# Two operand buffers of a TensorE kernel start 32 bytes lower in their partition

## The chip, the core and the metric

The kernel runs on one core of a Trainium2 chip. The metric is the device time of one execution in microseconds. Three runs of the kernel before took 1187.24 to 1188.97 us, median 1188.03 us.

## The reference

Two transformer-like blocks run one after the other over one sequence of 256 tokens with 1,024 features, all in fp32.

```python
# first block
u = rms_norm(h, norm_mix)
z, xbc, dt_raw, q_a, c_kv, k_rope, gate_ssd, gate_mla = split_cols(u @ w_in, IN_SPLITS)
y_ssd = ssd_branch(z, xbc, dt_raw, ...) @ w_ssd_out
y_mla = mla_branch(q_a, c_kv, k_rope, positions, ...) @ w_mla_out
h = h + (sigmoid(gate_ssd) * y_ssd + sigmoid(gate_mla) * y_mla) @ w_o
h = h + memory_cross_attention(rms_norm(h, norm_xattn), rms_norm(mem, norm_mem), ...)
h = h + hierarchical_moe(rms_norm(h, norm_moe), ...)     # 32 experts, top 2 of one group
x = rms_norm(h, norm_final)
# second block
hq, hf, hi, hg, sq, sk, sv = split(rmsnorm(x, attn_pre_norm) @ w_in_2)
mix = concatenate([rmsnorm(hgrn2_mix(hq, hf, hi)) * silu(hg), rmsnorm(stick_breaking_mix(sq, sk, sv))]) @ w_out_2
h = x + rmsnorm(mix, attn_post_norm)
gate, up = split(rmsnorm(h, ffn_pre_norm) @ w_gate_up_2)
h = h + rmsnorm((silu(gate) * up) @ w_down_2, ffn_post_norm)
out = h + (p @ ple_proj_2) * sigmoid(h @ ple_gate_2)
```

## The kernel before

Activations lie with features on the 128 partitions and tokens along them: a buffer of the shape [128, 8, 256] holds 8 groups of 128 features of all 256 tokens, so one row of 256 tokens is 1,024 bytes of a partition. The large products are made with three matmuls in place of one. A factor x is split into an upper part, x rounded to the format fp32r, and a lower part, the rest; ScalarE (ACT) writes the upper part by a copy (line 1180) and VectorE (DVE) the lower one by a subtraction (line 1757 for weights, 1763 for activations). The product is upper by upper, plus weight upper by activation lower, plus weight lower by activation upper.

Weights come in pieces of up to 2,048 floats a partition. SyncE's queue (SP) loads piece after piece into raw0 to raw3, ACT writes its upper part to one of three buffers whi0 to whi2, DVE its lower part to one of wlo0 to wlo2, and TensorE uses it and so gives the buffers back. DVE and ACT split the pieces ahead of TensorE, between their other work. The order of the work is written out by hand in one program per engine (`pe_program`, `act_program`, `dve_program`, `pool_program`, `sp_program`), with waits on semaphores between them.

**XUh and XUl** hold the upper and lower part of the normed activations that go into the first product of each stage. TensorE reads them in `triple`, called by `chunk` once for each half (128 outputs) of a piece:

```python
for k in range(kt):
    pe.matmul(ps, h(k), xh(k), start=start and k == 0, stop=False, ...)     # L436
    pe.matmul(ps, h(k), xl(k), start=False, stop=False, ...)                # L437
    t = pe.matmul(ps, l(k), xh(k), start=False, stop=stop and k == kt - 1, ...)  # L438
```

Here h and l are the piece's upper and lower part, 128 columns of weights (the stationary operand), and xh(k) = XUh[:, k, :] and xl(k) = XUl[:, k, :] are streamed, 256 columns. With kt = 8 that makes 24 matmuls for a half. `chunk` runs so for the mix projections and gates of the first block (from 19 to 245 us and, for gate_mla, up to 384 us), for the projections of the second block (812 to 922 us), for the gate and up products of its feed-forward layer (969 to 1144 us), and for ple_gate (from 1163 us). In `chunk_tok` (the second block's values, 862 to 898 us) the roles are changed: XUh and XUl are the weights, and whi and wlo are streamed. Other products run through the same three lines with other buffers: YAh, XCh, OAh, MXh, MMh, XVh, OXh, MIh, PTh, ffnah.

In the profile's rows `ps<-XUh,whi` names the output, then the streamed operand, then the weights.

During the experts (562 to 810 us) XUh and XUl aren't in use. Their place is taken by XT (the tokens, 8 KB), Y (the outputs of a group of experts, 4 KB) and sphs0 and sphs1 (1 KB each). XT (line 1096) and Y (line 1153) are weights of fp32 matmuls there.

Buffers are placed by `sb`, which without an offset takes the next free byte and rounds the size up to 64 bytes:

```python
def sb(name, shape, dt, offset=None):
    ...
    if offset is None:
        offset = at[0]
        at[0] += (n + 63) // 64 * 64
    return nc.alloc_sbuf_tensor_at(name, shape, dt, offset=offset)
```

In the built program every large buffer starts at a multiple of 64 bytes: whi0 at 49,280 of its partition, XUh at 98,624, XUl at 106,816, H at 115,008. Ahead of XUh lies `flag`, 16 bytes from 98,560 on, so the 32 bytes below XUh are free.

Of the kernel before, what the change touches and what calls it, by code (L numbers as in the profile page):

```python
# [5 lines left out]
F32R = mybir.dt.float32r  # L6
# [5 lines left out]
KB = 1024  # L12
# [212 lines left out]
def build(nc, I, out, parts, vectors):  # L225

    at = [(nc.sbuf_base + 63) // 64 * 64]

    def sb(name, shape, dt, offset=None):
        n = 1 if dt == U8 else 4  # L230
        for s in shape[1:]:
            n *= s
# [4 lines that stand above are left out]
# [3 lines left out]
    hi = [sb(f"whi{i}", [128, PIECE], F32R) for i in range(3)]  # L240
    lo = [sb(f"wlo{i}", [128, PIECE], F32R) for i in range(3)]
    lb, flag = sb("lb", [128, 32], F32), sb("flag", [128, 4], I32)
    xu_at = at[0]
    XUh, XUl = sb("XUh", [128, 8, 256], F32R), sb("XUl", [128, 8, 256], F32R)
    H = sb("H", [128, 8, 256], F32)
    t_at = at[0]
    T8, T8b = sb("T8", [128, 8, 256], F32), sb("T8b", [128, 8, 256], F32)
# [2423 lines left out]
```

How the kernel before makes its waits and increments, by code:

```python
    def wait_ge(self, sem, n):  # L58
        if sem is None:
            assert isinstance(self.e, Idle), n
            return
        key = sem.name
        if self.done.get(key, 0) < n:
            self.done[key] = n
            self.e.wait_ge(sem, n)
# [366 lines left out]
        def triple(ps, h, l, xh, xl, kt, ready=None, start=True, stop=True, loose=False):  # L432
            for k in range(kt):
                if ready is not None:
                    w.wait_ge(*ready(k))
                pe.matmul(ps, h(k), xh(k), start=start and k == 0, stop=False, skip_group_check=loose)
                pe.matmul(ps, h(k), xl(k), start=False, stop=False, skip_group_check=loose)
                t = pe.matmul(ps, l(k), xh(k), start=False, stop=stop and k == kt - 1, skip_group_check=loose)
            return t
# [1 line left out]
        def chunk(name, c, xh, xl, kt, ready, nt=2, banks=bank, among=(0, 1, 2, 3, 4, 5, 6, 7), between=None):  # L441
            i = first[name] + c
            h, l = split_of(i)
            ps, free = banks.take(name, c, among=among)
            w.wait_ge(*free)
            w.wait_ge(*at_("split", i))
            for j in range(nt):
                if j and between is not None:
                    between()
                t = triple(ps[:, 256 * j:256 * j + 256], lambda k: h[:, k, 128 * j:128 * j + 128], lambda k: l[:, k, 128 * j:128 * j + 128],
                           lambda k: xh[:, k, :], lambda k: xl[:, k, :], kt, ready)
            t.then_inc(*did("w_used", "used", i))
```

## Time and profile before

| | |
|---|---|
| three runs, median (lowest to highest) | 1188.03 us (1187.24 to 1188.97) |
| the profiled execution, its own time | 1185.96 us |
| its span, first to last instruction | 1184.2 us |
| mean granted TensorE clock, share of full speed | 0.947 |
| TensorE busy (matmuls) | 1040.6 us, 88% |
| VectorE busy | 639.5 us, 54% |
| ScalarE busy | 528.2 us, 45% |
| HBM read | 234.45 MB |

The engines run side by side, so their busy times don't add up. A matmul's duration in the trace runs from its start to a modelled end and overlaps the next ones; the time from one start to the next is what a matmul costs in a stream. Granted clock is the share of TensorE's 2.4 GHz that it was given.

### The profile page before, as it was taken

What the parts mean: (1) busy time and instruction counts of PE and PEld (TensorE: products, weight loads), DVE (VectorE), ACT (ScalarE), POOL (GpSimd) and SP (SyncE); (2) the same over time, 40 slices, a digit from 0 to 9 for tenths busy, and PEclk for the clock granted to TensorE, in tenths of its full rate; (3) what the DMA queues carried; (4) which work ended last, traced back from release to release, by engine and by line L of the source; (5) the groups of instructions that cost most, each with busy time, mean ns of one, the idle gap of its engine ahead of it and who ended that gap; (6) DMA issues with size and microseconds to landing.
All of it is one profiled execution on the core that took longest, in us unless ns stands there. A gap on an engine that the chain in (4) does not pass through costs nothing.

```text
span 1184.2 us, 19472 instructions
## 1 busy us (share of the span) xinstructions
PE 1040.6 (88%) x8600; PEld 951.4 (80%) x8600; DVE 639.5 (54%) x822; ACT 528.2 (45%) x712; POOL 7.8 (1%) x13
## 2 busy tenths in 40 slices
PE   3999997799978989997698777679999989999998
PEld 3999885799978889987665444448999879999998
DVE  6697656765554587444311111107996556555556
ACT  4476557564654556351211011116755555444444
POOL 0000000000000000000000000000000000000000
PEclk9999998899999999998599888889999989999999
DMA  6564321143502355369079999995432315555540
GB/s 259 178 213 180 111 104 72 71 159 135 214 36 72 136 185 186 135 264 417 41 306 421 421 420 420 420 415 221 172 143 72 151 75 214 200 188 178 212 145 37
DMA packets 34247, 236.80 MB, mean 200 GB/s; under 512 B 3952, under 2 KB 4592, under 8 KB 6256
## 3 DMA queue, kind: packets, MB, share of 16 engines
q1 hardware_dynamic: 32976, 232.54, 51.3%
q0 software_dynamic: 464, 2.12, 0.5%
q8 instruction: 70, 1.15, 0.4%
q10 hardware_dynamic: 720, 0.85, 0.2%
q14 instruction: 17, 0.14, 0.0%
HBM read 234.45 MB, written 1.05 MB: 199 GB/s over the span
## 4 chain that ended last, share of the span: by engine, by line
PE 61%; DVE 14%; DMA 12%; ACT 8%; issue 3%; SPq 1%; DVEq 0%; ACTq 0%
PE ps L436 14%; PE ps L437 14%; PE ps L438 14%; DMA wr<-in_c_weights 7%; DVE wlo L1757 4%; DMA raw<-in_c_weights 3%; ACT whi L1180 3%; PE ps L1110 2%; DMA xlo<-in_c_weights 2%; PE ps L484 2%; SPq L2602 1%; PE ps L553 1%; PE ps L1096 1%; PE ps L858 1%; PE ps L1138 1%
## 5 line engine op out<-in xcount | busy, mean ns | idle before, releaser
L1757 DVE TENSOR_TENSOR wlo<-raw,whi 128x2048 fp32r<-128x2048 f32 (+2 forms) x123 | 274.3, 2233 | 135.1 <-ACT whi L1180 135.1
L436 PE MATMUL ps<-XUh,whi 128*128 128x256 f32 x1032 | 293.3, 284 | 14.0 <-DVE XUl L1763 7.9
L437 PE MATMUL ps<-XUl,whi 128*128 128x256 f32 x1032 | 288.8, 280 | 0.0
L438 PE MATMUL ps<-XUh,wlo 128*128 128x256 f32 x1032 | 288.6, 280 | 0.0
L1180 ACT ACTIVATE whi<-raw 128x2048 fp32r<-128x2048 f32 (+2 forms) x123 | 228.6, 1861 | 71.4 <-PE ps L438 70.6
L436 PEld LDWEIGHTS ps<-XUh,whi 128*128 128x128 f32 x1032 | 195.9, 190 | 17.4 <-issue 14.9
L437 PEld LDWEIGHTS ps<-XUl,whi 128*128 128x128 f32 x1032 | 196.1, 190 | 0.9 <-issue 0.8
L438 PEld LDWEIGHTS ps<-XUh,wlo 128*128 128x128 f32 x1032 | 196.6, 190 | 0.0
L1110 PE MATMUL ps<-wr,Xg 128*32 128x256 f32 x400 | 51.2, 457 | 21.9 <-DMA raw<-in_c_weights 12.2
L2564 DVE SCALAR_TENSOR_TENSOR sphs<-sphs,wsl,ps 128x256 f32<-128x256 f32 x8 | 3.8, 480 | 112.9 <-ACT sphs L1728 112.9
L1110 PEld LDWEIGHTS ps<-wr,Xg 128*32 128x32 f32 x400 | 25.2, 131 | 37.9 <-issue 32.9
L1728 ACT ACTIVATE sphs<-ps 128x256 f32<-128x256 f32 x8 | 3.1, 383 | 113.3 <-PE ps L1110 113.3
L2569 DVE COPY Y<-ps 128x512 f32<-128x512 f32 x8 | 5.5, 692 | 82.1 <-PE ps L1138 82.1
L436 PE MATMUL ps<-ffnah,whi 128*128 128x256 f32 x176 | 49.1, 279 | 0.7 <-DVE wlo L1757 0.7
L437 PE MATMUL ps<-ffnal,whi 128*128 128x256 f32 x176 | 49.2, 280 | 0.0
L438 PE MATMUL ps<-ffnah,wlo 128*128 128x256 f32 x176 | 49.1, 279 | 0.0
L1110 PE MATMUL ps<-raw,Xg 128*32 128x256 f32 x256 | 36.6, 451 | 7.1 <-DMA wr<-in_c_weights 6.4
L436 PE MATMUL ps<-YAh,whi 128*128 128x256 f32 x128 | 36.3, 283 | 0.1
L1110 PE MATMUL ps<-xhi,Xg 128*32 128x256 f32 x160 | 23.2, 454 | 14.8 <-DMA xlo<-in_c_weights 14.8
L438 PE MATMUL ps<-YAh,wlo 128*128 128x256 f32 x128 | 35.8, 279 | 0.0
L437 PE MATMUL ps<-YAl,whi 128*128 128x256 f32 x128 | 35.7, 279 | 0.0
L436 PEld LDWEIGHTS ps<-ffnah,whi 128*128 128x128 f32 x176 | 33.1, 188 | 0.8 <-issue 0.8
(531 smaller groups left out, 2401.3 us busy)
## 6 DMA issues: line engine op xcount, KB each, us to landing
raw<-in_c_weights SPq DMA_DIRECT2D x142, 1024.0 KB, 4.9
wr<-in_c_weights SPq DMA_DIRECT2D x39, 1024.0 KB, 26.7
xhi<-in_c_weights SPq DMA_DIRECT2D x15, 1024.0 KB, 26.1
xlo<-in_c_weights SPq DMA_DIRECT2D x15, 1024.0 KB, 26.4
T<-in_c_weights SPq DMA_DIRECT2D x5, 1024.0 KB, 27.0
raw<-in_c_weights SPq DMA_DIRECT2D x4, 576.0 KB, 3.6
raw<-in_c_weights SPq DMA_DIRECT2D x3, 512.0 KB, 6.6
H<-in_c_x SPq DMA_DIRECT2D x1, 1024.0 KB, 5.6
```

The source lines that it names most:

```text
L436: pe.matmul(ps, h(k), xh(k), start=start and k == 0, stop=False, skip_group_check=loose)
L437: pe.matmul(ps, h(k), xl(k), start=False, stop=False, skip_group_check=loose)
L438: t = pe.matmul(ps, l(k), xh(k), start=False, stop=stop and k == kt - 1, skip_group_check=loose)
L484: t = pe.matmul(ps[:, 256 * j:256 * j + 256], wt[:, k, 128 * j:128 * j + 128], x[:, k, :], start=n == j == 0, stop=n == 7, skip_group_chec ...
L553: t = pe.matmul(ps[:, 256 * j:256 * j + 256], ident[0:32, hd:hd + 1].broadcast_to([32, 128]), acT[0:32, :])
L858: t = pe.matmul(ps[:, 128 * hd:128 * hd + 128], x, x)
L1096: t = pe.matmul(ps[:, 128 * r:128 * r + 128], XT[:, j, 128 * k:128 * k + 128], Pg[s][:, j, :], start=j == 0, stop=j == 1)
L1110: t = pe.matmul(ps[o:o + 32, 256 * n:256 * n + 256], x[:, k, o:o + 32], plain_of(expert[name, 4 * g + e])[:, k, :], start=k == 0, stop=k == 7)
L1138: t = pe.matmul(dps[f][o:o + 32, :], a[:, k, o:o + 32], plain_of(i)[:, k, 512 * f:512 * f + 512], start=k == 0, stop=k == 1)
L1180: return act.activation(out, in_, ACT.Copy, **kw)
L1757: dve.tensor_tensor(l[:, 0:n], r, h[:, 0:n].bitcast(F32), ALU.subtract).then_inc(*did("w_lo", "split", i))
L2602: sp.dma_start(raw_of(i), I["c_weights"][o:o + 128 * kt * n].rearrange("(p n) -> p n", p=128)).then_inc(*did("%s%d" % home[i], "loaded", i ...
```

## The change

XUh and XUl are placed by an explicit offset, 32 bytes below the place they had, and 16 KB are set aside, so that H and all that follows stay where they were.

```diff
     lb, flag = sb("lb", [128, 32], F32), sb("flag", [128, 4], I32)
-    xu_at = at[0]
-    XUh, XUl = sb("XUh", [128, 8, 256], F32R), sb("XUl", [128, 8, 256], F32R)
+    xu_at = at[0] - 32
+    XUh = sb("XUh", [128, 8, 256], F32R, xu_at)
+    XUl = sb("XUl", [128, 8, 256], F32R, xu_at + 8 * KB)
+    at[0] += 16 * KB
     H = sb("H", [128, 8, 256], F32)
```

XUh now starts at byte 98,592 and XUl at 106,784. The four buffers that share their place are given by the same name and move along:

```python
XT = sb("XT", [128, 2, 1024], F32, xu_at)
Y = sb("Y", [128, 1024], F32, xu_at + 8 * KB)
shs = [sb(f"sphs{i}", [128, 256], F32, xu_at + (12 + i) * KB) for i in range(2)]
```

Every engine has the same instructions in the same order as before.

## Rows read from the trace of the kernel before

**Rows 1.** The page, busy time of each engine, then TensorE in 40 slices and its granted clock (tenths)

```profile
PE 1040.6 (88%) x8600; PEld 951.4 (80%) x8600; DVE 639.5 (54%) x822; ACT 528.2 (45%) x712; POOL 7.8 (1%) x13
PE   3999997799978989997698777679999989999998
PEclk9999998899999999998599888889999989999999
```

**Rows 2.** The page, the chain that ended last, by line

```profile
PE ps L436 14%; PE ps L437 14%; PE ps L438 14%; DMA wr<-in_c_weights 7%; DVE wlo L1757 4%; DMA raw<-in_c_weights 3%; ACT whi L1180 3%; PE ps L1110 2%; DMA xlo<-in_c_weights 2%; PE ps L484 2%; SPq L2602 1%; PE ps L553 1%; PE ps L1096 1%; PE ps L858 1%; PE ps L1138 1%
```

**Rows 3.** The page, costliest groups (line, engine, streamed operand, weights | busy us, mean ns | idle)

```profile
L436 PE MATMUL ps<-XUh,whi 128*128 128x256 f32 x1032 | 293.3, 284 | 14.0 <-DVE XUl L1763 7.9
L437 PE MATMUL ps<-XUl,whi 128*128 128x256 f32 x1032 | 288.8, 280 | 0.0
L438 PE MATMUL ps<-XUh,wlo 128*128 128x256 f32 x1032 | 288.6, 280 | 0.0
```

**Rows 4.** Busy time in stretches, instructions that use XUh alone

```profile
860.00:930.00 70.00, 36.41 (x199) 30.41 (x199) 0.00 (x0) 0.00 (x0) 1.00 0.26 91
969.00:1184.00 215.00, 134.07 (x768) 117.03 (x768) 2.49 (x4) 2.52 (x4) 1.00 0.48 172
```

**Rows 5.** Chain by line, stretches 0:128, 128:206, 206:250, 324:384, 812:860, 860:930

```profile
by line: PE ps L436 23.2%; PE ps L438 22.5%; PE ps L437 22.5%; DMA raw<-in_c_weights 7.6%; ACT whi L1180 4.5%; DVE wlo L1757 3.6%; issue 2.9%; PE ps L544 2.7%; DVE T8b L1796 1.8%; DVE XUl L1763 1.0%; DVE T L1906 0.7%; DVE T L1904 0.7%; DVE 
...
by line: PE ps L553 17.9%; DVE wlo L1757 16.9%; ACT M L1327 12.0%; DVE M L1978 9.1%; PE ps L578 5.9%; ACT M L1330 4.9%; ACT CE L1325 4.9%; DVE CE L1981 4.4%; PE ps L575 4.1%; PE ps L558 3.4%; ACT L1177 3.3%; PE ps L574 3.1%; DVE xs L1948 2.
...
by line: DVE xs L1948 10.4%; ACT whi L1180 8.2%; DVE YAl L1763 8.2%; PE ps L436 6.8%; issue 6.2%; PE ps L437 6.1%; PE ps L438 5.8%; PE ps L578 5.5%; DVE T8b L1796 5.3%; PE ps L472 4.6%; DVE T L1779 4.4%; PE ps L575 3.9%; ACT T8b L1180 3.6%;
...
by line: ACT Pm L1424 13.2%; ACT Pm L1423 11.0%; PE ps L664 9.7%; PE ps L665 9.5%; DVE sm L2066 7.6%; DVE Pm L2071 5.7%; PE ps L659 5.5%; PE ps L660 5.2%; DVE Pm L2059 5.0%; DVE Pm L2070 4.6%; DVE Pm L2060 4.4%; PE ps L680 4.4%; DVE sm L206
...
by line: PE ps L436 13.5%; PE ps L437 13.0%; PE ps L438 12.8%; DVE wlo L1757 11.5%; issue 8.2%; DVE hb L2284 4.8%; PE ps L858 3.7%; PE ps L868 3.7%; PE ps L491 3.6%; PE ps L484 2.7%; DVE hz L1829 2.7%; DVE he L2282 2.6%; DVE he L2274 2.6%; 
...
by line: PE ps L436 17.1%; PE ps L437 16.8%; PE ps L438 16.7%; PE ps L858 15.3%; PE ps L902 5.0%; PE ps L925 5.0%; PE ps L892 3.3%; PE ps L880 2.8%; PE ps L916 2.8%; ACT whi L1180 2.6%; PE ps L904 2.6%; PE ps L903 2.5%; ACT L1177 1.8%; PE p
```

**Rows 6.** Timeline of TensorE (start us, us), first and last of 457 on XUh, XUl

```profile
61.00 0.28 PE L436 MATMUL ps<-XUh,whi 128*128 128x256 f32 x1
...
114.71 0.28 PE L436 MATMUL ps<-XUh,whi 128*128 128x256 f32 x1
```

**Rows 7.** Timeline of TensorE, first and last of 142 on XUh, XUl

```profile
1164.25 0.28 PE L438 MATMUL ps<-XUh,wlo 128*128 128x256 f32 x1
...
1180.23 0.28 PE L438 MATMUL ps<-XUh,wlo 128*128 128x256 f32 x1
```

**Rows 8.** Timeline of TensorE at 239 us, and the stretch's granted clock (column PEclk)

```profile
239.16 0.41 PE L438 MATMUL ps<-XUh,wlo 128*128 128x256 f32 x1
239.37 0.41 PE L436 MATMUL ps<-XUh,whi 128*128 128x256 f32 x1
...
237.90:240.00 2.10, 2.10 (x8) 1.58 (x7) 1.88 (x1) 1.67 (x4) 0.00 (x0) 0.50 0.03 8
```

**Rows 9.** VectorE, lines 1927 and 2564 (duration min/median/max)

```profile
L1927 DVE SCALAR_TENSOR_TENSOR T8b<-ps,vec,T8b x72: 469/474/482, 55.0 to 115.2; 128x253 f32<-128x253 f32 x24, 128x254 f32<-128x254 f32 x24, 128x255 f32<-128x255 f32 x24
...
L2564 DVE SCALAR_TENSOR_TENSOR sphs<-sphs,wsl,ps x8: 479/480/481, 602.7 to 793.9; 128x256 f32<-128x256 f32 x8
```

**Rows 10.** Who writes XUl, and the weight load of Y

```profile
L1763 DVE TENSOR_TENSOR XUl<-XP,XUh x8: 684/686/687, 811.9 to 965.8; 128x512 fp32r<-128x512 f32 x8
...
L1153 PEld LDWEIGHTS ps<-PT,Y x128: 186/190/192, 621.9 to 805.6; 128*128 128x128 f32 x128
```

**Rows 11.** Timeline of TensorE, 512 streamed columns

```profile
310.75 0.40 PE L436 MATMUL ps<-whi,XCh 128*128 128x512 f32 x1
...
311.45 0.40 PE L436 MATMUL ps<-whi,XCh 128*128 128x512 f32 x1
```

**Rows 12.** Groups by form, XUh and MMh as weights

```profile
L436 PE MATMUL ps<-whi,XUh 128*128 128x256 f32 x64 | 18.3, 285 | 0.0
...
L436 PE MATMUL ps<-whi,MMh 128*128 128x256 f32 x64 | 17.9, 280 | 1.2 <-DVE wlo L1757 1.2
```

## The prediction

> **What bounds the kernel now.** I read the page first: TensorE is busy for 88% of the span, and from the 28th of its 40 slices on at 8 or 9 tenths, at the full granted clock [rows 1]. The chain that ended last agrees: three lines of TensorE, 436 to 438, hold 42% of it [rows 2]. These are the three matmuls of `triple`. Of their groups the largest by far stream XUh or XUl, the two moved buffers: 1,032 matmuls on each line, 3,096 in all, with no idle time ahead of two of the three lines [rows 3]. So the question is what one matmul that streams 256 columns (1,024 bytes per partition) out of XUh or XUl costs, start to start. Its "mean ns of one" (280) doesn't tell, since matmuls overlap. The timeline does.
>
> From 61.00 to 114.71 us stand 456 of them without a break: 53.71 us / 456 = 117.8 ns each [rows 6]. From 1164.25 to 1180.23 us, same buffers and same granted clock, stand 141: 113.3 ns each [rows 7]. **Two rates** thus exist at full clock. Which one holds isn't a matter of the address, since both come with the same ones; a run keeps its rate until a stop or a change of buffers. Reading the timeline through by runs, 1,488 matmuls that use XUh or XUl keep 117.8, 1,752 keep 113.3, and 48 lie where the clock is down.
>
> Where the granted clock is 0.50 (1.2 GHz) the same matmuls follow each other by 0.21 us: 239.16 and 239.37 [rows 8]. That is 256 columns / 1.2 GHz = 213.3 ns, one column per cycle and nothing lost. At 2.4 GHz the same would be 106.7 ns. Measured is 113.3, which is 106.7 x 17/16. With 512 streamed columns three matmuls need 0.70 us (310.75 to 311.45), 233 ns each [rows 11], twice 117, so what is lost grows with the columns and isn't a fixed sum per instruction. My reading: at full clock TensorE is held up by the delivery of the streamed operand, in portions, with one cycle lost for each 16 columns, and 16 columns are 64 bytes.
>
> **The change part by part.** It removes and adds no instruction and moves none in order; it moves addresses. XUh starts at byte 98,624 of its partition before, a multiple of 64, and at 98,592 after, 32 past one. The same holds for XUl and for every row of 1,024 bytes in them.
>
> *Streamed rows.* A row that begins on a 64-byte boundary covers 16 portions; one that begins in the middle of one covers 17. No row of this trace streams a wide operand from such a start, so the cost is bounded: below by nothing lost, above by the half rate of rows 8, where a column takes twice as long. The nearest row is the 113.3 ns of rows 7, which I divide: 113.3 / 16 = 7.08 ns per portion. I take one more portion, **+7.08 ns** a matmul (113.3 becomes 120.4, or 117.8 becomes about 125).
>
> The Trainium skill speaks against it: "SBUF — State Buffer", section Specifications, gives 16-byte cachelines, and 98,592 is a multiple of 16, so a row covers 64 lines either way and by that rule the change costs nothing; no row here can show its line size. "TensorE: Matmul & The Clock Gate", section Back-to-back issue gap, puts the warm gap at 256 columns at 262 cycles, with no term for the address, which would also leave the sum at zero; the trace's 113.3 ns are 272 cycles, so it doesn't tell all.
>
> *How many of them are on the path.* By stretch, from the chain by line [rows 5] and the counts of XUh [rows 4] (XUh stands in two of three matmuls, so its count times 1.5 is all):
> - 0 to 128 us: lines 436 to 438 hold 68.2% of 128 us = 87.3 us, / 117.8 ns = 741.
> - 128 to 206 us and 324 to 384 us: they aren't among the listed lines. There the recurrence and the softmax set the pace on DVE and ACT, and the matmuls on XUh fill TensorE's waits: 0.
> - 206 to 250 us: 18.7% of 44 us = 8.2 us: 70.
> - 812 to 860 us: 39.3% of 48 us = 18.9 us: 160.
> - 860 to 930 us: XUh is counted 199 times; 2 x 64 of them as weights [rows 12], the other 71 times 1.5 make 106.
> - 969 to 1184 us: 768 x 1.5 = 1,152, TensorE without gaps of note.
>
> The sum is 2,229 matmuls x 7.08 ns = **15.8 us**. If all 3,096 counted it would be 21.9.
>
> *XUh and XUl as weights.* In 192 matmuls of `chunk_tok` they are the loaded operand. The weight load runs beside the matmul ahead of it, and MMh in the same role gives the same mean (280 ns against 285) [rows 12]. One portion more, 7.08 x 192 = 1.4 us, is the upper end, 0 the lower; I take 0. XT and Y, which start at the same moved address, are only weights of fp32 matmuls whose weight load, 190 ns [rows 10], lies beside the matmul ahead in the same way: 0 too.
>
> *DVE and ACT.* VectorE has misaligned operands already: the convolution (line 1927) writes and reads T8b from 4, 8 and 12 bytes past the boundary, 253 to 255 elements in 474 ns, against 480 ns for 256 elements from a boundary [rows 9]. So no cost; the upper bound, a sixteenth of the writing of XUl (8 x 0.69 us for the second block's two norms [rows 10], and about as much again elsewhere), is under 1 us. ScalarE has no such row; the same bound.
>
> *DMA.* No transfer touches the moved buffers; weights go to raw and the split ones to whi and wlo, which stay. What is late next where the path is TensorE's is again TensorE.
>
> The profiled execution took 1185.96 us (its span 1184.2), 2.07 under the median of 1188.03. 1185.96 + 15.8 = 1201.8; against the median 1188.03 + 15.8 = **1203.8 us**. The forecast's own range, from half a portion to one and a half with more or fewer on the path, is 1196 to 1214.
>
> **The rivals.**
> *Nothing changes* (1188, within 2.4 us). The portions may be smaller than 64 bytes, or the 17th may be fetched while the weights change. For it: both rates exist at one address, so what is lost may be no matter of addresses. Against it: the loss is exactly 1/16. This is also the case in which the change doesn't do what its words promise.
>
> *All at the slow rate.* The offset could tie all to 117.8: about 1,247 of the 2,229 on the path run fast now, x 4.45 ns = 5.5 us, 1193.6.
>
> *Faster.* The two rates may come from the weight read and the streamed read meeting in the same place: both begin on a multiple of 64. Shifting one by 32 bytes may part them. The place is the same 2,229 matmuls; if all keep 113.3, the 982 slow ones and the 192 of `chunk_tok` gain 4.45 ns each, 5.2 us: 1182.8. If the loss vanishes too (106.7), 982 x 11.1 + 1,247 x 6.6 ns = 19.1 us: 1168.9. It decides at a start-to-start time under 113 ns. For it: the rate changes on entering other buffers. Against it: with 512 columns the weights are half as much per column and the loss per column is the same [rows 11].
>
> *Much slower.* If each portion straddled a boundary and were read twice, up to the half rate: (213.3 - 115.3) ns x 2,229 = 218 us, 1406. I keep it as a tail.
>
> **How the numbers follow.** Forecast 0.46, all slow 0.11, much slower 0.05, nothing 0.20, faster 0.18 (0.10 near 1183, 0.08 below). A measurement of this kernel tells about 0.2% (2.4 us) from no change. So faster 0.18, same 0.20, slower 0.62. The range runs from 1182, which takes in the first faster case, to 1214, and leaves out 0.05 above and 0.08 below.
>
> **What would show it.** In the timeline around 1170 us: 120 ns start to start is the forecast, 113.3 nothing, 117.8 the slow rate, 107 the faster rival. The other streams (YAh, OAh, MMh, ffnah) must keep their two rates. The waits of 128 to 206 us should shrink where fillers grew. I am wrong if XU's matmuls keep their rates, or if they lengthen and the span doesn't.

## The result, and the profile after

The changed kernel takes 1191.84 us (median of 18 runs, 1189.09 to 1196.53) against 1187.82 us for the kernel before (18 runs, 1184.14 to 1192.89). The ratio is 1.0034 [1.0020, 1.0047], so it is 4.0 us slower, with 2.4 to 5.6 us as the interval. The forecast was 15.8 us slower: the sign held, the size was four times too large. The profiled execution took 1193.84 us (span 1192.0).

The page of the kernel after: busy time of each engine, TensorE and its granted clock in 40 slices (they answer to [rows 1]), the chain by line, and three of the costliest groups (busy us, mean ns | idle):

```profile
PE 1053.9 (88%) x8600; PEld 964.0 (81%) x8600; DVE 639.5 (54%) x822; ACT 528.0 (44%) x712; POOL 7.8 (1%) x13
...
PE   3999997799988989997698777769999989999998
...
PEclk9999988999989889999599888789999989999999
...
PE ps L438 15%; PE ps L439 15%; PE ps L440 15%; DMA wr<-in_c_weights 7%; DMA raw<-in_c_weights 3%; DVE wlo L1759 3%; ACT whi L1182 3%; PE ps L1112 2%; DMA xlo<-in_c_weights 2%; PE ps L486 2%; PE ps L555 1%; SPq L2604 1%; PE ps L1098 1%; PE ps L860 1%; PE ps L1140 1%
...
L438 PE MATMUL ps<-XUh,whi 128*128 128x256 f32 x1032 | 296.5, 287 | 13.1 <-DVE XUl L1765 7.9
L439 PE MATMUL ps<-XUl,whi 128*128 128x256 f32 x1032 | 292.1, 283 | 0.0
L440 PE MATMUL ps<-XUh,wlo 128*128 128x256 f32 x1032 | 291.8, 283 | 0.0
```

Lines are two higher than before, so 438 to 440 are the old 436 to 438. VectorE is busy 639.5 us as before and ScalarE 528.0 against 528.2; all that grew is TensorE, by 13.3 us of busy time, and its three lines hold 45% of the chain in place of 42% [rows 2]. The mean of one matmul is 3 ns longer [rows 3]. As before, the rate is read start to start in the timeline. First and last of four unbroken stretches of the kernel after:

```profile
61.04 0.28 PE L440 MATMUL ps<-XUh,wlo 128*128 128x256 f32 x1
...
114.79 0.28 PE L440 MATMUL ps<-XUh,wlo 128*128 128x256 f32 x1
...
976.17 0.28 PE L438 MATMUL ps<-XUh,whi 128*128 128x256 f32 x1
...
979.29 0.28 PE L440 MATMUL ps<-XUh,wlo 128*128 128x256 f32 x1
...
1103.08 0.28 PE L440 MATMUL ps<-XUh,wlo 128*128 128x256 f32 x1
...
1111.53 0.28 PE L440 MATMUL ps<-XUh,wlo 128*128 128x256 f32 x1
...
1174.00 0.28 PE L438 MATMUL ps<-XUh,whi 128*128 128x256 f32 x1
...
1187.88 0.28 PE L438 MATMUL ps<-XUh,whi 128*128 128x256 f32 x1
```

They hold 453, 26, 72 and 117 steps: 118.7, 120.0, 117.4 and 118.6 ns. So there are three rates now, 117.3, 118.7 and 120.0, where before there were 117.8 [rows 6] and 113.3 [rows 7]; 113.3 is gone from these buffers. Over all unbroken runs on XUh and XUl at full clock the mean rose from 115.2 to 118.0 ns, **+2.8 ns** where 7.08 was forecast. Streams of YAh, OAh, XVh and OXh kept 117.8, 117.8, 117.8 and 113.3. One stream that wasn't moved changed too: the first one of ffnah, 48 matmuls from 989 us on, went from 113.3 to 117.8 (e11 below is about such changes).

Where the time came from is best seen in the last sixth, which is TensorE alone (91% of its chain is the three lines). The first XUh matmul of that stage, before and after, and the last one of the kernel after:

```profile
1011.70 0.28 PE L436 MATMUL ps<-XUh,whi 128*128 128x256 f32 x1
```

```profile
1015.75 0.28 PE L438 MATMUL ps<-XUh,whi 128*128 128x256 f32 x1
...
1188.11 0.28 PE L440 MATMUL ps<-XUh,wlo 128*128 128x256 f32 x1
```

Before, it goes on to 1180.23 [rows 7]: 168.53 us. After, 172.36 us: +3.83. In between lie 912 matmuls on XUh and XUl, whose mean went from 113.36 to 117.56 ns, and 912 x 4.20 ns = 3.83. Every nanosecond added to a matmul is in the time here. In the first 128 us, where 117.8 was the rule, 741 x (118.72 - 117.04) ns gives 1.2 us, and the profiled pair is 0.4 us apart when that stretch ends.

The profiled pair differs by 7.9 us, more than the medians. Part of the rest is the granted clock (0.941 against 0.947 on average): from 154 to 159 us the kernel after was at half clock, where the one before had the full one. Nothing ties this to the change, since over many runs the mean granted clock is the same, 0.943 for the kernel after (18 runs) and 0.943 for the kernel before (the 31 runs beside e7 to e10). Windows of after, columns as in [rows 8] (PE, PEld, DVE, ACT, POOL, then PEclk):

```profile
154.00:159.00 5.00, 5.00 (x24) 5.00 (x25) 2.76 (x11) 3.91 (x11) 0.00 (x0) 0.50 0.02 5
```

### The profile page after: what moved, and what is told of

It reads as the page before. It is cut to its first block, busy times and chain, and to the rows that moved or that the text cites. A ratio compares the mean times of both kernels' runs of the same rounds, so it can differ in the third digit from the quotient of the medians.

```text
span 1192.0 us, 19472 instructions
## 1 busy us (share of the span) xinstructions
PE 1053.9 (88%) x8600; PEld 964.0 (81%) x8600; DVE 639.5 (54%) x822; ACT 528.0 (44%) x712; POOL 7.8 (1%) x13
## 4 chain that ended last, share of the span: by engine, by line
PE 64%; DMA 12%; DVE 12%; ACT 7%; issue 3%; SPq 1%; DVEq 0%; ACTq 0%
PE ps L438 15%; PE ps L439 15%; PE ps L440 15%; DMA wr<-in_c_weights 7%; DMA raw<-in_c_weights 3%; DVE wlo L1759 3%; ACT whi L1182 3%; PE ps L1112 2%; DMA xlo<-in_c_weights 2%; PE ps L486 2%; PE ps L555 1%; SPq L2604 1%; PE ps L1098 1%; PE ps L860 1%; PE ps L1140 1%
## 5 line engine op out<-in xcount | busy, mean ns | idle before, releaser
L438 PE MATMUL ps<-XUh,whi 128*128 128x256 f32 x1032 | 296.5, 287 | 13.1 <-DVE XUl L1765 7.9
L439 PE MATMUL ps<-XUl,whi 128*128 128x256 f32 x1032 | 292.1, 283 | 0.0
L440 PE MATMUL ps<-XUh,wlo 128*128 128x256 f32 x1032 | 291.8, 283 | 0.0
L1112 PE MATMUL ps<-wr,Xg 128*32 128x256 f32 x400 | 53.6, 480 | 22.4 <-DMA raw<-in_c_weights 14.1
```

Of the source, the lines that this page charges most:

```text
L439: pe.matmul(ps, h(k), xl(k), start=False, stop=False, skip_group_check=loose)
L1112: t = pe.matmul(ps[o:o + 32, 256 * n:256 * n + 256], x[:, k, o:o + 32], plain_of(expert[name, 4 * g + e])[:, k, :], start=k == 0, stop=k == 7)
```

## The experiments

**The theory I had** (portions of 64 bytes, one more for a start between two) says that the streamed operand's own start decides. **Its rival** after the result: what counts is where the streamed operand lies relative to the weights, since the change moved that distance too. In the kernel before, whi and wlo start at 128 modulo 256 and XUh and XUl at 64, a distance (streamed minus weights) of 192 modulo 256; in the changed one it is 160. YAh, OAh, MMh, XVh and the other streamed buffers start at 192 modulo 256, a distance of 64.

### Moving the weights: e1_both32 and e2_w32

e1 keeps the changed XUh and XUl and moves whi and wlo 32 bytes up. e2 moves the weights in the same way and puts XUh and XUl back on their 64-byte boundary.

```diff
-    hi = [sb(f"whi{i}", [128, PIECE], F32R) for i in range(3)]
+    spare_at = at[0] + 32
+    hi = [sb(f"whi{i}", [128, PIECE], F32R, spare_at + i * 8 * KB) for i in range(3)]
...
+    xu_at = end_at + 160      # e1: 98,592
+    xu_at = end_at + 192      # e2: 98,624
```

> XUh and XUl stay where the changed kernel has them (32 past a multiple of 64) and the split weights whi and wlo are moved by 32 bytes as well, so that streamed operand and weights again lie a multiple of 64 apart (98,592 and 49,312: 64 mod 128 of distance, as before the change 98,624 and 49,280 had). Distance theory (what counts is where the two reads lie to each other): the matmuls on XUh and XUl are back at 113.3 and 117.8 ns start to start, and the streams of YAh, OAh, MMh, ffnah, still on a boundary but now 32 off against the weights, take the rates of the changed kernel (117.3 to 120.0). Boundary theory (a streamed row off a multiple of 64 costs): XUh and XUl stay at 117.3 to 120, the others stay at 113.3 and 117.8. Time: about 1190 by either.

> XUh and XUl as before the change, whi and wlo alone moved by 32 bytes. Distance theory: all streams against whi and wlo (XUh, YAh, OAh, MMh, XVh, OXh, ffnah) leave 113.3 and 117.8 and take 117.3 to 120.0, some 5,700 matmuls; slower than the changed kernel, 1193 to 1198. Boundary theory for the streamed operand: nothing changes but for chunk_tok, where whi and wlo are the streamed ones: 1188.

One thing in the expectation of e1 is wrong: with the weights up by 32 and XUh down by 32 the distance is not restored but 64 less than before, 128 modulo 256. The run is read by the true distance. In both expectations the rates for the other streams are wrong as well: their distance became 32, not 160, and at 32 they took 116.7 and 117.8 ns, not 117.3 to 120.0.

e1: 1194.14 us (5 runs), ratio 1.0069 [1.0036, 1.0102]; XU at 118.7 and 120.0, mean 118.8. e2: 1192.25 us (8 runs), ratio 1.0045 [1.0015, 1.0075]; XU at 117.3, 118.7 and 120.0, mean 118.1. **e2 is the telling one:** XUh and XUl lie where they lay before, on the boundary, and yet they show the three rates of the changed kernel and nearly its time. What e2 shares with the changed kernel is the distance, 160. In both runs streams of other buffers, which didn't move, changed as well (OXh from 113.3 to 116.7 in both, OAh from 117.8 to 116.7 in e1, but not in e2, where it kept 117.8): their distance went from 64 to 32. The theory of portions falls here. One way out stays, that weights off a boundary cost something, since e2 moved them off; e9 and e10 below close it.

### The distance by itself: e3_grid and e5_dist

Two programs of their own that leave out all of the reference's work. Each runs blocks of 96 matmuls in the kernel's pattern (upper by upper, upper by lower, lower by upper; 256 columns, fp32r), one block after the other with a stop between. e3 has starts of 0, 32, 64, 96, 4 and 16 bytes for the streamed operand and 0, 32, 64 for the weights; e5 has every multiple of 32 up to 480 and four starts of the weights, one of them twice.

```python
for j in (0, 1, 0, 1):
    for k in range(8):
        c = dw // 4 + 256 * k + 128 * j
        t = f(pe, p, W[:, c:c + 128], W[:, 2048 + c:2176 + c], k)   # f streams x[dx:], three matmuls
```

> A program of its own, none of the reference's work: TensorE alone streams 256 columns of fp32r in the kernel's pattern of three (upper by upper, upper by lower, lower by upper), 96 matmuls a block, for streamed operands that start 0, 4, 16, 32, 64 or 96 bytes past a multiple of 256 and weights 0, 32 or 64 past one, each pair twice. Distance theory: the mean start to start depends on the difference alone, so (streamed 32, weights 32) equals (0, 0) or (64, 64), and (0, 32) equals (32, 0) within 0.5 ns. Boundary theory: the rows with streamed 0 and 64 are at 113.3 or 117.8 whatever the weights, all others at 117.3 or more. Portion theory of the prediction (7.08 ns more) would give 120.4 at every streamed start off a multiple of 64; the changed kernel's 117.3 speaks against it already.

> A program of its own, none of the reference's work: 96 matmuls a block as before, streamed operand 0 to 480 bytes past a multiple of 512 in steps of 32 (one source line each), weights at 0, 32, 128, 0 again and 64. In the first grid the distance of the streamed start from the weights' start decided, by multiples of 128: 0 gave 120.0 ns, 64 gave 117.8 or 113.3, 32 gave 116.7. Distance theory by 128: the rows repeat every 128 bytes. Distance theory by 256: they repeat every 256 only; the kernels say so, since with the weights moved (e2_w32) XUh lies 160 off by 256 and had 117.3 to 120 while the others lie 32 off and had 116.7. So at a distance of 160 I expect about 118.0, at 32 and 33 times that pattern 116.7. Boundary theory would have all rows off a multiple of 64 alike at any weights; the first grid speaks against it.

The timeline of eight of e5's blocks in a row, weights at 0, the streamed operand at 0, 32, ... 224, then of two later ones; a row is one block (start, duration to the end of the last, ... x matmuls):

```profile
38.94 11.76 PE L27 MATMUL ps<-x,w 128*128 128x256 f32 x96 [0.38 <-DVE scr L126]
51.15 11.47 PE L31 MATMUL ps<-x,w 128*128 128x256 f32 x96 [0.45 <-DVE scr L126]
62.94 11.57 PE L35 MATMUL ps<-x,w 128*128 128x256 f32 x96 [0.32 <-DVE scr L126]
74.90 11.77 PE L39 MATMUL ps<-x,w 128*128 128x256 f32 x96 [0.38 <-DVE scr L126]
87.12 11.66 PE L43 MATMUL ps<-x,w 128*128 128x256 f32 x96 [0.45 <-DVE scr L126]
99.10 11.53 PE L47 MATMUL ps<-x,w 128*128 128x256 f32 x96 [0.32 <-DVE scr L126]
111.02 11.17 PE L51 MATMUL ps<-x,w 128*128 128x256 f32 x96 [0.38 <-DVE scr L126]
122.63 11.62 PE L55 MATMUL ps<-x,w 128*128 128x256 f32 x96 [0.45 <-DVE scr L126]
...
134.57 11.78 PE L59 MATMUL ps<-x,w 128*128 128x256 f32 x96 [0.32 <-DVE scr L126]
...
206.65 11.17 PE L83 MATMUL ps<-x,w 128*128 128x256 f32 x96 [0.32 <-DVE scr L126]
```

The duration runs to the end of the block's last matmul, and the first step after each stop takes about 220 ns whatever the distance; start to start, behind these first steps, the first block keeps 120.0 ns and the seventh, at 192, 113.3. The row at 134.57 is a streamed start of 256: 11.78 again, as at 0; the one at 206.65 is 448 = 256 + 192: 11.17 again. Ten blocks stand for each distance, start to start in ns:

| distance mod 256 | 0 | 32 | 64 | 96 | 128 | 160 | 192 | 224 |
|---|---|---|---|---|---|---|---|---|
| rate (blocks) | 120.0 (10) | 116.7 (10) | 117.8 (6), 113.3 (4) | 120.0 (10) | 118.7 (7), 120.0 (3) | 117.3 (7), 118.7 (3) | 113.3 (8), 117.8 (2) | 118.3 (10) |

The ten of a distance come from eight pairs of starts (two of them run twice), on and off a boundary of 64, so the start alone doesn't decide and the distance does, with a period of 256 bytes (one of 128 is excluded: 0 and 128 differ, as do 32 and 160, and 96 and 224; 64 and 192 share their two rates). The kernels' rates fit the table (192 before, 160 after, 64 for YAh and the others) with two exceptions, both higher than it says: at 160 a few streams of XUh keep 120.0 (976.17 us above), and at 32 some keep 117.8 (OAh in e2).

e3 agrees in all blocks but one, and that one shows the same thing: at distance 32, streamed start 32 and weights at 0, it had 117.8 the first time and 116.7 the second. It also ran one pair of distance 192 (streamed 0, weights 64) twice, behind the same block and a stop, first and last start of each:

```profile
221.56 0.38 PE L41 MATMUL ps<-xa,wc 128*128 128x256 f32 x1 [0.45 <-DVE scr L78]
...
232.45 0.28 PE L43 MATMUL ps<-xa,wc 128*128 128x256 f32 x1
...
438.11 0.39 PE L41 MATMUL ps<-xa,wc 128*128 128x256 f32 x1 [0.45 <-DVE scr L78]
...
449.40 0.28 PE L43 MATMUL ps<-xa,wc 128*128 128x256 f32 x1
```

That is 10.89 and 11.29 us for 95 steps, 113.3 and 117.8 ns once past the first ones. So the starts fix which rates are possible, but not which of them is taken.

A streamed start 4 bytes past a multiple of 16 is dearer still in e3: 123.4, 120.8 and 122.2 ns with weights at 0, 32 and 64, where a start 16 bytes past the boundary had 116.7, 117.1 and 119.1.

The 4-byte case is what the Trainium skill lets one expect ("SBUF — State Buffer", section Specifications: 16-byte cachelines): by that figure such a row touches 65 lines in place of 64. That the lines are the reason isn't shown. By the same figure a shift of 32 would cost nothing, and there the trace disagrees, since 113.3 became 117.3 to 120.0 with 64 lines either way.

### Which instructions have it: e4_forms

The same in blocks of 48 with 512 columns in fp32r, 512 in bf16 and 128 in fp32r, each with four streamed starts and three starts of the weights. It leaves out all of the reference's work.

```diff
-    pe.matmul(p[:, 0:256], hi, xh(k), ...)
+    pe.matmul(p[:, 0:512], w[:, 128*k:128*k+128], x[:, o+256*k:o+256*k+512], ...)   # L43, and L40 in bf16
+    pe.matmul(p[:, 0:128], w[:, 128*k:128*k+128], x[:, o+128*k:o+128*k+128], ...)   # L46
```

> A program of its own, none of the reference's work: the same question for 512 streamed columns of fp32r, for 512 of bf16 and for 128 of fp32r, starts 0, 32, 64, 96 against weights at 0, 32, 64. If the delivery of the streamed operand binds only at 4 bytes a column, bf16 needs 213.3 ns for its 512 columns at any start (one per cycle at 2.4 GHz), while fp32r with 512 columns needs twice what 256 need and shows the same dependence on the start. If addresses matter for bf16 as well, its rows differ by over 1 ns.

The timeline, a block in a row; xa, xb, xc, xd start at 0, 32, 64, 96, wa at 0 and wc at 64 (so xa with wc is distance 192); ba and bb are bf16:

```profile
90.32 11.19 PE L43 MATMUL ps<-xa,wa 128*128 128x512 f32 x48 [0.45 <-DVE scr L81]
101.83 11.46 PE L43 MATMUL ps<-xb,wa 128*128 128x512 f32 x48 [0.32 <-DVE scr L81]
113.68 11.26 PE L43 MATMUL ps<-xc,wa 128*128 128x512 f32 x48 [0.38 <-DVE scr L81]
...
184.10 11.47 PE L43 MATMUL ps<-xa,wc 128*128 128x512 f32 x48 [0.38 <-DVE scr L81]
...
242.16 10.53 PE L40 MATMUL ps<-bb,ba 128*128 128x512 bf16 x48 [0.32 <-DVE scr L81]
...
362.35 5.58 PE L46 MATMUL ps<-xa,wa 128*128 128x128 f32 x48 [0.45 <-DVE scr L81]
```

Start to start: fp32r with 512 columns 226.7 ns at distance 0 (three blocks), 228.9 at 64 (two), 233.3 at 32, 96, 192 and 224 (seven); bf16 with 512 columns 215.8 in all twelve blocks; fp32r with 128 columns 111.6 to 111.7 in all twelve. The rate varies with the address only where fp32r is streamed in 256 columns or more. At 128 columns something else sets the pace, since half the columns take nearly the time of 256.

**With 512 columns the order of the distances is another one.** The expectation, the same dependence on the start as with 256, didn't hold: 0, the slowest distance there, is the fastest here, and 192, which there has the lowest rate, is among the slowest. The kernels bear this out with their own 512-column stream (whi and wlo streamed against XCh and XCl, 24 matmuls): at distance 192 it has 233.4 ns before and after the change (before: ten steps from 310.75 to 313.08 us), and in e7 below, where its distance is 64, 228.8 (ten steps from 310.78 to 313.07).

The Trainium skill ("TensorE: Matmul & The Clock Gate", Back-to-back issue gap) gives 518 cycles as the isolated gap at 512 columns, 215.8 ns at 2.4 GHz, which the bf16 blocks match; it has no term for fp32r's 11 to 18 ns on top, and none for the address.

### Which operand meets which: e6_pair

Separate starts for the streamed upper and lower part and for the upper and lower weights (64 combinations, streamed upper part at 0), then 32, 64 and 96 columns of weights in place of 128. It leaves out all of the reference's work.

```diff
-    hi, lo = W[:, c:c + 128], W[:, 2048 + c:2176 + c]
+    hi, lo = wh[:, dw//4 + c:dw//4 + c + m], wl[:, ((dw + do) % 128)//4 + c:((dw + do) % 128)//4 + c + m]
```

> A program of its own, none of the reference's work: upper and lower streamed parts and upper and lower weights each in a buffer of its own, all 64 combinations of starts by 32 bytes, then weights of 32, 64 and 96 columns in place of 128. If what is lost at full clock is a meeting of the weight read with the streamed read, it shrinks with fewer weight columns: with 32 columns (a quarter of the read) the time nears 106.7 + a quarter of 10 = about 109 ns and depends less on the start. If it is the streamed read alone that binds (the reading in the prediction: one cycle for each 64 bytes), 32 columns of weights still need 113.3. Some of the 64 combinations may keep 113.3 on every entry; none is expected at 106.7.

The 64 combinations lie between 115.6 and 120.2 ns, but for one at 113.3, the one in which all four starts give the distance 192. So the rate isn't that of one operand pair. With fewer weight columns I had expected the loss to shrink with the amount of weights read, to about 109 ns; it didn't: 32 columns gave 113.3 to 117.8, 64 columns 113.3 to 119.1, 96 columns 116.0 to 118.2, by the start of the weights. The order of the distances changes here too: with 64 columns of weights, distance 0 had 113.3 and 192 had 119.1 (one block each), so the table above holds for 128 columns of weights and 256 streamed ones. A collision whose cost grows with the bytes of the weights isn't what happens. What in the chip the distance acts on stays open.

### Distances set in the kernel: e7 to e10

If the table holds, the kernel's rates can be chosen. e7_all192 places XUh and XUl, and by the weights' start all other streams too, at 192. e8_xu32 puts XUh and XUl at distance 32, with a start 32 bytes past a boundary. e9_xu0 gives them distance 0 with a start on a multiple of 128. e10_off192 gives them distance 192 with both starts off the boundary. To find room, e7, e8 and e10 load 824 of the 896 columns of cst (the rest isn't used).

```diff
-    XUh, XUl = sb("XUh", [128, 8, 256], F32R), sb("XUl", [128, 8, 256], F32R)
+    spare_at, xu_at = raw_end + 16512, raw_end + 64       # e7: weights 65,792, XUh 49,344
+    spare_at, xu_at = raw_end + 0, raw_end + 49184        # e8: 49,280 and 98,464
+    spare_at, xu_at = raw_end + 16480, raw_end + 32       # e10: 65,760 and 49,312
+    XUh, XUl = sb("XUh", ..., xu_at), sb("XUl", ..., xu_at + 8 * KB)
...
+    xu_at = end_at + 0                                    # e9: weights 49,280, XUh 98,432
```

> All starts on multiples of 64, but the weights whi and wlo and XUh, XUl placed so that every streamed activation (XUh as well as YAh, OAh, MMh, XVh, MIh, ffnah) starts 192 past the weights by a multiple of 256, the distance at which the second grid had 113.33 ns throughout. Distance theory: the 1,980 matmuls of the other streams that keep 117.8 ns before go to 113.3 for the most part, about 1,500 of them on the path: 4.45 ns x 1,500 = 6.7 us less, 1181; chunk_tok and the attention values (weights streamed) lie at 64 and may go to 117.8. XUh keeps its two rates. Boundary theory: nothing changes, 1188.

> XUh and XUl again 32 bytes past a multiple of 64, but on the other side of the weights: 32 past them by 256 (the changed kernel has 160). Distance theory: start to start 116.7 ns throughout for the 3,096 (the changed kernel: 117.3, 118.7 and 120.0), so about 1.3 ns x 2,229 = 3 us under the changed kernel, 1189, and near the kernel before, with the same offset from a boundary. Boundary theory: as the changed kernel, 1192.

> XUh and XUl at byte 98,432, a multiple of 64 and of 128, at distance 0 from the weights by 256. Distance theory: 120.0 ns throughout (118.7 in places), the slowest distance of the grids, so slower than the changed kernel though on the boundary: 115.3 to about 119.7 x 2,229 = 9.8 us more, 1197. Boundary theory: as before the change, 113.3 and 117.8, 1188.

> XUh, XUl and the weights all off a multiple of 64 by 32, at the distance they had before the change (192 by 256). Distance theory: XUh back at 113.3 and 117.8; the other streams, now at 224 off the weights, at 118.3. Boundary theory: XUh at 117.3 or more, the others at 113.3 and 117.8. The time should be near 1189 by the first (XUh as before, the others 0.5 ns slower).

"XU" and "others" are mean rates in ns over the unbroken runs at full clock (others: all remaining streams through the three lines):

| kernel | XU start mod 64 | XU distance, others' | XU | others | us | ratio |
|---|---|---|---|---|---|---|
| before | 0 | 192, 64 | 115.2 | 117.1 | 1187.82 | 1 |
| the change | 32 | 160, 64 | 118.0 | 117.2 | 1191.84 | 1.0034 [1.0020, 1.0047] |
| e2 | 0 | 160, 32 | 118.1 | 117.2 | 1192.25 | 1.0045 [1.0015, 1.0075] |
| e1 | 32 | 128, 32 | 118.8 | 116.9 | 1194.14 | 1.0069 [1.0036, 1.0102] |
| e9 | 0 | 0, 64 | 120.0 | 117.5 | 1197.65 | 1.0064 [1.0042, 1.0087] |
| e8 | 32 | 32, 64 | 117.0 | 116.7 | 1190.72 | 1.0000 [0.9979, 1.0022] |
| e10 | 32 | 192, 224 | 114.0 | 118.2 | 1189.67 | 0.9993 [0.9973, 1.0013] |
| e7 | 0 | 192, 192 | 115.6 | 116.0 | 1186.38 | 0.9964 [0.9941, 0.9987] |

Times are compared by a row's ratio only: the kernel before ran beside each, with a median of 1187.05 us beside e1 and e2 and 1189.33 beside e7 to e10, and the ratio comes from the runs side by side, not from the two medians. Means of rates shift by 0.1 to 0.2 ns with the choice of runs counted. The expectation of e7 misreads e5: two of the ten blocks at distance 192 had 117.8. In e8 XUh and XUl kept 116.7 for the most part, and 117.8 to 120.0 in the rest. The last stage's last stretch, timeline of e9 (100 steps, 120.0 ns), of e8 (103 steps, 116.6) and of e10 (106 steps, 113.3):

```profile
1177.95 0.28 PE L440 MATMUL ps<-XUl,whi 128*128 128x256 f32 x1
...
1189.95 0.28 PE L441 MATMUL ps<-XUh,wlo 128*128 128x256 f32 x1
```

```profile
1168.88 0.28 PE L438 MATMUL ps<-XUl,whi 128*128 128x256 f32 x1
...
1180.89 0.28 PE L439 MATMUL ps<-XUh,wlo 128*128 128x256 f32 x1
```

```profile
1175.38 0.28 PE L437 MATMUL ps<-XUh,whi 128*128 128x256 f32 x1
...
1187.39 0.28 PE L438 MATMUL ps<-XUl,whi 128*128 128x256 f32 x1
```

e9 lies on a boundary of 128 and has the slowest XU of all, 120.0 ns throughout. e10 lies off a boundary of 64 by 32 bytes, streamed operand and weights alike, and its XU is faster than before, 114.0 ns against 115.2. Boundary and rate are thereby parted from each other twice, in both directions. That e10's time equals that of the kernel before is a sum of two things, XU faster by 1.2 ns and the others slower by 1.1, so it is the rates that tell. e7 is faster than the kernel before, by 0.36%. Its gain is not on XUh: its last stretch runs at 117.8 where before had 113.3, while YAh, OAh and MIh came down from 117.8 to 113.3. Other streams at the same distance of 192 gained nothing: XVh, most of MMh and all but the first stream of ffnah stayed at 117.8, and that stream and OXh went up from 113.3 to 117.8. Timeline of e7, a stretch on YAh (45 steps, 113.3 ns), then the last one on XUh (103 steps, 117.8):

```profile
265.69 0.28 PE L438 MATMUL ps<-YAl,whi 128*128 128x256 f32 x1
...
270.79 0.28 PE L438 MATMUL ps<-YAl,whi 128*128 128x256 f32 x1
...
1170.87 0.28 PE L439 MATMUL ps<-XUh,wlo 128*128 128x256 f32 x1
...
1183.00 0.28 PE L437 MATMUL ps<-XUh,whi 128*128 128x256 f32 x1
```

The changes of rate times the number of matmuls of each stream, were all of them on the path, give e7 a gain of about 2.0 us. Measured is 0.36%, 4.3 us; 2.0 lies within its interval (1.5 to 7.0), so the two agree, but the interval is too wide to confirm the size. The expected 6.7 us rested on all these streams taking 113.3.

### Two rates at one distance: e11_entry

A distance of 192 gives 113.3 or 117.8. e11, once more without any of the reference's work, enters 72 matmuls of distance 192 in four ways, ten times each.

```python
if first:                    # x32, x64 or x96: 24 matmuls of that distance, no stop behind them
    stream(pe, p, first)
stream(pe, p, x192); stream(pe, p, x192); return stream(pe, p, x192)
```

> A program of its own that leaves out all of the reference's work: 40 blocks of fp32r matmuls of 256 columns, weights on a multiple of 256 bytes. In each block 72 matmuls stream from a start 192 bytes further on, the distance that has shown two rates (113.3 and 117.8 ns). They are entered in four ways, each ten times: after a stop of TensorE, or without a stop behind 24 matmuls of distance 32, 64 or 96. The theory that the way in decides (what is queued or in flight when the stream begins): each of the four ways gives one rate, the same in all its ten blocks, and at least two ways differ. The rival, that it falls by chance at each entry: both rates in every way, in shares that differ little. A second rival, that the rate belongs to the place of the weights and was moved by something else in the kernel: one rate, 113.3 ns, in all 40. In every case the 24 matmuls ahead keep 116.7 (distance 32), 113.3 or 117.8 (64) and 120.0 ns (96).

The timeline: 24 matmuls of distance 32 (line 31), 64 (35) or 96 (39), then without a stop 72 of distance 192 (line 27); the row at 101.16 is an entry after a stop, those at 110.05 and 112.96 the other case of distance 32:

```profile
41.98 3.07 PE L31 MATMUL ps<-x,w 128*128 128x256 f32 x24 [0.45 <-DVE scr L85]
44.89 8.64 PE L27 MATMUL ps<-x,w 128*128 128x256 f32 x72
...
77.56 3.14 PE L39 MATMUL ps<-x,w 128*128 128x256 f32 x24 [0.45 <-DVE scr L85]
80.54 8.34 PE L27 MATMUL ps<-x,w 128*128 128x256 f32 x72
89.20 3.09 PE L35 MATMUL ps<-x,w 128*128 128x256 f32 x24 [0.32 <-DVE scr L85]
92.13 8.64 PE L27 MATMUL ps<-x,w 128*128 128x256 f32 x72
101.16 8.45 PE L27 MATMUL ps<-x,w 128*128 128x256 f32 x72 [0.38 <-DVE scr L85]
110.05 3.07 PE L31 MATMUL ps<-x,w 128*128 128x256 f32 x24 [0.45 <-DVE scr L85]
112.96 8.34 PE L27 MATMUL ps<-x,w 128*128 128x256 f32 x72
```

After distance 96 all ten settle at 113.3 (8.34 us), after distance 64 all ten at 117.8 (8.64 us). After a stop the first step takes 222 ns, and all ten are at 113.3 within a handful of steps. After distance 32 seven stay at 117.8 and three go to 113.3. In those three the 24 matmuls ahead ran in another rhythm at nearly the same mean: steps of 118, 120, 113 and 116 ns over and over, where the seven had 117, 116 and 117. So what runs ahead decides, and for distance 32 something finer than its distance does; neither chance in equal shares nor one rate for all fits. It isn't the whole account: in e3 a pair of distance 192 took 113.3 once and 117.8 the other time, both behind a stop and the same block. That a run, once in, kept its rate through all its remaining matmuls here is what the kernels show too. Which entry gives which rate in the kernel's own sequence wasn't worked out.

## Why the prediction was right or wrong

**What bounds the kernel: right.** TensorE's three lines in the chain went from 42 to 45%, and in the last sixth the added nanoseconds came out whole in the time.

**"I take one more portion, +7.08 ns a matmul (113.3 becomes 120.4, or 117.8 becomes about 125)": this step failed.** The mean went up by 2.8 ns, not 7.08, and nothing reached 125. The mechanism under it, portions of 64 bytes counted from the operand's own start, is refuted by e9 (on the boundary, 120.0 ns, 0.64% slower), by e10 (off it, 114.0 ns) and by e2 (on it, with the changed kernel's rates). In its place stands the distance between streamed operand and weights modulo 256, which the change took from 192, where the lowest rate (113.3) occurs, to 160, where 117.3 is the least. The reading that led there was "Which one holds isn't a matter of the address, since both come with the same ones". Both rates do occur at one address, but it doesn't follow that the address is without effect: it fixes which rates are possible, and the way in chooses between them. The loss of exactly 1/16 is one of several (113.3, 116.7, 117.3, 117.8, 118.7, 120.0), and I built on it alone.

**The count of matmuls on the path: a little high.** 2,229 x 2.8 ns = 6.3 us. Taking the change of rate by stretch (1.2 us to 128, 0.3 at 206 to 250, 0.2 at 812 to 860, 0.3 at 860 to 930, 4.3 from 969 on) gives 6.4. Measured are 4.0 [2.4, 5.6], in e9 7.6 [5.0, 10.3] against 10.4 worked out in the same way. For the last stretch the count fits: from its first XUh matmul to its last, before 970.00 to 1180.23 us and after 973.77 to 1188.11, it is 4.1 us longer against the 4.3. The excess lies before it, as in the first 128 us (0.4 against 1.2); that some of those matmuls have slack which the chain by line doesn't show is likely, but no run shows which.

**XUh and XUl as weights: taken as 0, it was some tenths.** whi streamed against XUh went from 117.8 to 120.0 ns (distance 64 to 96), 192 x 2.2 ns = 0.4 us at most. The mean by form rose from 285 to 287 [rows 12]. The group of after, over its whole span:

```profile
L438 PE MATMUL ps<-whi,XUh 128*128 128x256 f32 x64 | 18.4, 287 | 0.0
```

**VectorE, ScalarE, DMA at 0: right.** VectorE's busy sum is the same to the tenth, and the write of XUl takes 683 ns in place of 686 [rows 10]. Its group by form, after:

```profile
L1765 DVE TENSOR_TENSOR XUl<-XP,XUh 128x512 fp32r<-128x512 f32 x8 | 5.0, 683 | 0.0
```

**The rivals.** "All at the slow rate" (5.5 us, 1193.6) came nearest in size, but not as written: the rates became 117.3, 118.7 and 120.0, and the slow runs changed too. "Faster" named the right thing, the weight read and the streamed read in relation to each other, and had the wrong sign for this shift. Its argument against (equal loss per column with 512 columns) excluded only a loss that grows with the weights, which e6 excludes too. The trace of the kernel before couldn't have settled it. XUh lay at distance 192 and all other streamed buffers at 64, and both distances show the same two rates (OXh 113.3 and OAh 117.8, both at 64); it took a run with another distance to see that it matters. The range, 1182 to 1214, held the time.

## What to carry to other kernels

Where back-to-back fp32r matmuls with 256 or more streamed columns bound a kernel, list the start of each streamed operand minus that of its weights modulo 256, beside its start-to-start time in the trace. With 256 streamed columns and 128 of weights that distance is worth up to 6% of a matmul here (113.3 to 120.0 ns); 192 and 64 can give 113.3 (192 did in 8 of e5's 10 blocks, 64 in 4), and 0 and 96 are the ones to avoid. For another shape measure anew: with 512 streamed columns 0 was the fastest (226.7 ns) and 192 among the slowest (233.3). Time the whole kernel afterwards: moving one operand changes the distance of all that meets it, and a distance with two rates can give the slower one, as e7 did on XUh. An address mod 64 by itself told nothing.

## What the runs showed that I had not expected

- The rate repeats with 256 bytes of distance between streamed operand and weights: 120.0, 116.7 (seldom 117.8), 117.8 or 113.3, 120.0, 118.7 or 120.0, 117.3 or 118.7 (in kernels also 120.0), 113.3 or 117.8, 118.3 ns for 0 to 224, with 256 streamed columns and 128 of weights.
- With 512 streamed columns it is 226.7 ns at 0, 228.9 at 64 and 233.3 at 32, 96, 192 and 224: another order.
- bf16 at 512 columns doesn't have it (215.8 ns at all starts), and fp32r at 128 columns neither, but there one matmul takes 111.7 ns, nearly as long as with 256 columns.
- At distance 192, 24 matmuls of distance 64 ahead leave 117.8 ns for the next 72, and 24 of distance 96 leave 113.3.
- A streamed start 4 bytes past a multiple of 16 costs 2.4 to 8.9 ns more than the nearest multiple of 32 below, by the start of the weights (123.4 against 120.0, 120.8 against 118.4, 122.2 against 113.3 or 117.8).
